# Fifty-four of the input-projection units computed in pairs as Strassen's 2x2 block product

## What is computed

```python
h = rmsnorm(x, norm_g)                                   # 1056 x 1024
p = jnp.einsum('btd,dn->btn', h, w_in)                   # 1024 -> 12296 columns
o_a = silu(a_z) * (a_b * causal_dwconv(a_c * a_u, buf_a, conv_a_w))          # 3 taps
o_r = silu(r_z) * head_norm(retention_chunked(rotary(r_q), rotary(r_k), r_v, s_ret))
conv_c = causal_dwconv(glu_v * sigmoid(glu_g), buf_c, conv_c_w) + conv_c_b   # 31 taps
o_c = silu(c_z) * silu(layernorm(conv_c, ln_c_g, ln_c_b))
o_m = silu(m_z) * head_norm(sigmoid(m_o) * mlstm_chunked(m_q, m_k, m_v, i_pre, f_pre, ...))
proj = jnp.einsum('btnw,nwd->btnd', stack([o_a, o_r, o_c, o_m]), w_br)       # 4 x (512 -> 1024)
gates = sigmoid(g_all.reshape(bsz, T, 4, 1024))
y = jnp.einsum('btd,de->bte', jnp.sum(gates * proj, axis=2), w_out)
out = rmsnorm(x + y, final_g)                            # and the new states
```

## Time and profile before

| | us |
|---|---|
| median of 3 runs | 1593.6 |
| lowest, highest | 1592.13, 1593.8 |
| the profiled execution, whole | 1592.14 |
| its span, first to last instruction | 1590.1 |
| TensorE busy | 1560.0 |
| VectorE busy | 817.2 |
| ScalarE busy | 415.8 |
| GpSimd busy | 385.3 |
| mean granted clock of TensorE, share of full | 0.995 |

### The profile page before, as it was taken

One profiled execution on the slowest core, in us unless ns is written; L12 is line 12 of the kernel. 1 busy time (PEld: TensorE's weight loads), 2 busy tenths in 40 slices (PEclk: granted clock), 3 DMA queues, 4 the chain that ended last, 5 costly groups with the idle time before them and its releaser, 6 DMA issues.

```text
span 1590.1 us, 24807 instructions
## 1 busy us (share of the span) xinstructions
PE 1560.0 (98%) x10217; PEld 1541.0 (97%) x10217; DVE 817.2 (51%) x1571; ACT 415.8 (26%) x756; POOL 385.3 (24%) x213
## 2 busy tenths in 40 slices
PE   8899999999999999999999999999999999999998
PEld 7899999999999999999999999989999999999998
DVE  6553342464100757644475469999947532332432
ACT  5332323233111223234211112121123322211311
POOL 4321212222221221221312322232322124431100
PEclk9999999999999999999999999999999999999999
DMA  4120211211111110221111211111111111221321
GB/s 166 56 96 27 69 45 52 82 34 51 54 47 47 48 64 27 71 72 27 56 47 40 71 44 44 57 47 40 47 42 47 40 54 41 87 77 49 103 84 70
DMA packets 27688, 92.34 MB, mean 58 GB/s; under 512 B 3624, under 2 KB 4152, under 8 KB 27448
## 3 DMA queue, kind: packets, MB, share of 16 engines
q1 hardware_dynamic: 22632, 73.35, 14.2%
q0 software_dynamic: 3744, 13.08, 2.4%
q10 hardware_dynamic: 1200, 4.33, 0.7%
...
## 4 chain that ended last, share of the span: by engine, by line
PE 86%; DVE 9%; issue 3%; ACT 1%; POOL 1%; DMA 0%; DVEq 0%; SPq 0%; ACTq 0%
PE bank L681 24%; PE bank L682 24%; PE bank L683 24%; DVE cc L1738 3%; PE bank L873 2%; PE bank L875 2%; PE bank L874 2%; DVE xt L1318 1%; PE pb L784 1%; PE tb L769 1%; PE pb L802 1%; PE pb L788 1%; PE tb L812 1%; PE pb L787 1%; PE tb L765 0%
## 5 line engine op out<-in xcount | busy, mean ns | idle before, releaser
L681 PE MATMUL bank<-h_hi,w_hi 128*128 128x352 f32 x2328 | 765.5, 329 | 12.6 <-POOL w_lo L1174 4.9
L683 PE MATMUL bank<-h_hi,w_lo 128*128 128x352 f32 x2328 | 749.9, 322 | 0.0
L682 PE MATMUL bank<-h_lo,w_hi 128*128 128x352 f32 x2328 | 749.7, 322 | 0.0
L1174 POOL TENSOR_TENSOR w_lo<-stage,w_hi 128x1024 fp32r<-128x1024 f32 (+1 forms) x131 | 286.3, 2185 | 814.5 <-ACT w_hi L903 814.3
L681 PEld LDWEIGHTS bank<-h_hi,w_hi 128*128 128x128 f32 x2328 | 439.6, 189 | 15.1 <-POOL w_lo L1174 5.4
L682 PEld LDWEIGHTS bank<-h_lo,w_hi 128*128 128x128 f32 x2328 | 440.4, 189 | 0.5
L683 PEld LDWEIGHTS bank<-h_hi,w_lo 128*128 128x128 f32 x2328 | 438.8, 188 | 0.0
L1738 DVE SCALAR_TENSOR_TENSOR cc<-ext,vc,cc 128x1024 f32<-128x1024 f32 x240 | 217.6, 948 | 19.0 <-ACT cc L1100 10.5
L903 ACT ACTIVATE w_hi<-stage 128x1024 fp32r<-128x1024 f32 (+1 forms) x131 | 124.6, 951 | 250.3 <-PE bank L683 239.4
L681 PE MATMUL bank<-o_hi,w_hi 128*128 128x352 f32 x384 | 124.7, 325 | 0.2 <-issue 0.2
L682 PE MATMUL bank<-o_lo,w_hi 128*128 128x352 f32 x384 | 123.3, 321 | 0.0
...
## 6 DMA issues: line engine op xcount, KB each, us to landing
...
```

The lines of the kernel that those rows point to most:

```text
L681: pe.matmul(out, hi, a_hi[:, k, tok(b)], start=(k == 0), stop=False)
L682: pe.matmul(out, hi, a_lo[:, k, tok(b)], start=False, stop=False)
L683: mm = pe.matmul(out, lo, a_hi[:, k, tok(b)], start=False, stop=(k == nk - 1))
L1174: pool.tensor_tensor(lo, stage[n % RING][:, 0:size], hi.bitcast(F32), ALU.subtract).then_inc(lo_done, 1)
```

## The change

**Pairs.** 43 units are computed as before, one after another. The other 54 form 27 pairs; the two units of a pair are the rows of a 2x2 block matrix, the halves of K its columns. The tokens are four blocks of 264 (`SBK`); the two blocks of one half (tp = 0, 1) are the columns of the other matrix. A pair is seven products of 128x512 weights with 512x264 columns for each tp, in the order P1, P6, P5, P7, P2, P4, P3: 14 steps of 12 matmuls. Kinds are "g" (two gates), "cvcg", "acau", "abaz" and "cz".

**Sums.** The combinations of h are made once by DVE (`comb`, `comb4`) and split by ACT and POOL; they take the place of acc and o in SBUF. The sums of weights are made by POOL for each pair (`sums`, four instructions), into `wsum` and in place in `stage`. Six weight slots of 128x512 (`t_hi`, `t_lo`) are a ring over the products. Part of the additions of results happens in PSUM: P2 adds onto P1's bank, P7 and P4 onto P6's, P3 onto P5's; before the next product is added, ACT or DVE must have read the bank (s1 after P1; u2 after P6; u3 and r22 after P7; r21 after P4; r12 after P3). TensorE waits for s1, u2, u3 and r22.

**DRAM.** Finished branch outputs go to DRAM (`store_out`, 16 of 128x1056), gates too (each 128x264 piece from SP as soon as its sigmoid is done). The merge of all 32 "p" units comes behind the pairs (`pblk`, three blocks of 352 each); gate pieces and outputs are loaded again there (`gload`, `oload`).

**Convolution.** One tap every 2.25 product steps, without a gap, steps 0 to 272 of 378; the layer norm's tasks lie at steps 276 to 321.

**Last stage.** Two halves of 512 columns in place of four quarters of 256.

```diff
+SBK = T // 4
...
-    tasks = {}
-    for g in range(1, 4):
-        tasks.update(spread(taps(g), 38 * g - 24, 1.25))
...
+    for what in (glu(1), None, conv_a(0), out_a(0), None, conv_a(1), glu(2), None, out_a(1), None, conv_a(2), glu(3),
+                 None, out_a(2), None, conv_a(3), None, out_a(3), None, None, None, None, None, out_c(0), out_c(2),
+                 None, None):
...
+    for g in range(4):
+        for i in range(1, CW):
+            tasks_at(68 * g + int(2.25 * (i - 1)), *([("tap0", g)] if i == 1 else []), ("tap", g, i))
...
+    cycle = [4, 2 * r0, 2 * r0 + 1, 2 * r1, 2 * r1 + 1, 5]
+    slot_of, prev = {}, {}
+    tiles = [("win", w, i) for w in range(nw) for i in range(7)]
+    for t, tile in enumerate(tiles):
+        slot_of[tile] = cycle[t % 6]
...
-            def split_lo(n):
-                src, dst = SPLITS[n]
-                size = src_of(src).shape[-1]
-                hi, lo = dst_of(dst, size)
-                pool.wait_ge(hi_done, n + 1)
-                pool.tensor_tensor(lo, stage[n % RING][:, 0:size], hi.bitcast(F32), ALU.subtract).then_inc(lo_done, 1)
...
+            def sums(w, pair):
+                first, second = stage_of(("win", w, 0)), stage_of(("win", w, 1))
+                if pair == 0:
+                    loaded(pool, ("win", w, 1))
+                    pool.tensor_tensor(wsum[0][:, :], second[:, 0:W], second[:, W:D], ALU.add).then_inc(wsum_done, 1)
+                    loaded(pool, ("win", w, 0))
+                    pool.wait_ge(wsum_done, 4 * w + 1)
+                    pool.tensor_tensor(wsum[1][:, :], wsum[0][:, :], first[:, 0:W], ALU.subtract).then_inc(wsum_done, 1)
+                else:
+                    pool.tensor_tensor(second[:, 0:W], first[:, 0:W], second[:, 0:W], ALU.subtract).then_inc(wsum_done, 1)
+                    pool.wait_ge(wsum_done, 4 * w + 2)
+                    pool.tensor_tensor(wsum[1][:, :], first[:, W:D], wsum[1][:, :], ALU.subtract).then_inc(wsum_done, 1)
+            def split(s):
+                item = SPL[s]
+                if item[0] == "win" and item[2] == P1:
+                    sums(item[1], 0)
+                hi, lo = dst_of(item)
+                pool.wait_ge(hi_done, s + 1)
+                pool.tensor_tensor(lo, split_src(item), hi.bitcast(F32), ALU.subtract).then_inc(lo_done, 1)
+                if item[0] == "win" and item[2] == P5:
...
+            def store_out(n, src):
+                pool.wait_ge(gated, n + 1)
+                pool.dma_start(o_rows[out_row(n)], src[:, :]).then_inc(o_out, 16)
...
+            def prod(w, i, tp):
+                if PAIRS[w][0] == "g" and signed("g", i):
+                    idx = SIG[(w, SIG_AT[i], tp)]
+                    unit, blk_, _ = GATE_OF[idx]
+                    sp.wait_ge(sgt_ready, idx + 1)
+                    sp.dma_start(g_rows[unit, :, sub(blk_)], sgt[idx % NT][:, :]).then_inc(g_out[idx % NT], 16)
...
+            def gload(x):
+                m, b = divmod(x, 3)
+                n, j = OUTS[m]
+                unit = n * KD + j
...
+                if piece_use(x) > 1:
+                    sp.wait_ge(piece_used, x - (6 if x < 48 else 5) + 1)
+                sp.dma_start(piece[piece_slot(x)][:, :], g_rows[unit, :, tok(b)]).then_inc(piece_in[piece_slot(x)], 16)
...
+            def prod(w, i, tp):
+                kind, n = PAIRS[w][0], 2 * w + tp + 1
+                tile = ("win", w, i)
+                if tp == 0:
+                    pe.wait_ge(lo_done, AT_SPLIT[tile] + 1)
+                nb = {P1: 0, P2: 0, P6: 2, P7: 2, P4: 2, P5: 4, P3: 4}[i] + tp
+                if i in (P1, P6, P5):
+                    take(nb)
+                if i == P6 and w == 0:
+                    pe.wait_ge(comb_lo, 12)
+                if i == P4 and w == 0:
+                    pe.wait_ge(t4_lo, 4)
+                if i == P7:
+                    pe.wait_ge(u2_done, n)
+                if i == P2:
+                    pe.wait_ge(s1_done, n)
+                    if kind == "g":
+                        last[nb] = (sgt_ready, SIG[(w, 11, tp)] + 1)
+                    else:
+                        e, c = FREED[("prod", w, i, tp)]
+                        last[nb] = (freed[e], c)
+                if i == P4:
+                    pe.wait_ge(u3_done, n)
+                    last[nb] = (r21_done, n)
+                if i == P3:
+                    pe.wait_ge(r22_done, n)
+                    last[nb] = (r12_done, n)
+                if i in (P6, P5, P7):
+                    c = {P5: 0, P6: 1, P7: 2}[i]
+                    a_hi, a_lo = (lambda k: c_hi[c][:, k, tp, :]), (lambda k: c_lo[c][:, k, tp, :])
+                else:
+                    k0, lr = {P1: (0, 0), P2: (4, 0), P4: (0, 1), P3: (4, 1)}[i]
+                    a_hi, a_lo = (lambda k: h_hi[:, k0 + k, sub(2 * tp + lr)]), (lambda k: h_lo[:, k0 + k, sub(2 * tp + lr)])
+                out, hi_t, lo_t = bank[nb][:, 0:SBK], t_hi[SLOT_OF[tile]], t_lo[SLOT_OF[tile]]
+                first = i in (P1, P6, P5)
+                for k in range(4):
+                    hi, lo = hi_t[:, k * P:(k + 1) * P], lo_t[:, k * P:(k + 1) * P]
+                    pe.matmul(out, hi, a_hi(k), start=(first and k == 0), stop=False, skip_group_check=True)
+                    pe.matmul(out, hi, a_lo(k), start=False, stop=False, skip_group_check=True)
+                    mm = pe.matmul(out, lo, a_hi(k), start=False, stop=(k == 3), skip_group_check=True)
+                mm.then_inc(blk_done, 1)
...
-                for q in range(4):
-                    out = ring[2 * (i % 4) + q // 2][:, 256 * (q % 2):256 * (q % 2) + 256]
+                for q in range(2):
+                    out = ring[2 * (i % 4) + q][:, :]
...
+            def prod(w, i, tp):
+                kind, info, _ = PAIRS[w]
+                n, done = 2 * w + tp + 1, DONE[("prod", w, i, tp)]
+                a_bank, b_bank, c_bank = (bank[2 * j + tp][:, 0:SBK] for j in range(3))
+                s1, u2, u3 = part[tp][:, :], part[2 + tp][:, :], part[4 + tp][:, :]
+                before = PAIRS[w - 1][0] if w else None
+                even, odd = sub(2 * tp), sub(2 * tp + 1)
+                if i == P6:
+                    dve.wait_ge(blk_done, done)
+                    dve.wait_ge(s1_done, n)
+                    if before == "g":
+                        dve.wait_ge(sgt_ready, SIG[(w - 1, 12, tp)] + 1)
+                    TT(u2, b_bank, s1, ALU.add).then_inc(u2_done, 1)
+                elif i == P7:
+                    dve.wait_ge(blk_done, done)
+                    if before in ("g", "cvcg"):
+                        dve.wait_ge(sgt_ready, SIG[(w - 1, 22, tp)] + 1)
+                    if w == 0:
+                        for s in gp_out:
+                            dve.wait_ge(s, 16 * (3 * PLAIN_GATES // 2))
+                    TT(u3, b_bank, s1, ALU.add).then_inc(u3_done, 1)
+                    dve.wait_ge(u3_done, n)
+                    TT(u3, c_bank, u3, ALU.add).then_inc(r22_done, 1)
...
+                elif i == P4:
+                    dve.wait_ge(blk_done, done)
+                    TT(s1, b_bank, s1, ALU.add).then_inc(r21_done, 1)
...
+                dve.wait_ge(blk_done, done)
+                TT(u2, c_bank, u2, ALU.add).then_inc(r12_done, 1)
+                if kind == "g":
+                    return
...
+            def pblk(m, b):
+                x = 3 * m + b
+                n, j = m // KD, OUTS[m][1]
+                ps, gate = bank[x % BANKS][:, 0:BLK], piece[piece_slot(x)][:, :]
+                dve.wait_ge(blk_done, DONE[("pblk", m, b)])
+                dve.wait_ge(piece_in[piece_slot(x)], 16 * piece_use(x))
+                if n == 0:
+                    own(TT(acc[:, j, tok(b)], ps, gate, ALU.mult))
+                    own.wait()
                     dve.sem_inc(freed["V"], 1)
-                    if b == 2:
-                        dve.wait_ge(olo_done, 8 + g)
...
-    wo = arr(w_out)[0].reshape(2, 4, P, 4, 256).transpose(3, 0, 2, 1, 4).reshape(8, P, D)
+    wo = arr(w_out)[0].reshape(4, 2, P, 2, 512).transpose(3, 0, 2, 1, 4).reshape(8, P, D)
```

1091 lines of the change are left out of this document (751 added, 340 removed).

## The result

The changed kernel takes **1675.97 us** (median of four runs, 1674.34 to 1678.09) against 1593.62: the ratio is 1.052, 95% interval 1.0501 to 1.0538. The prediction gave 1668 us, within 1588 to 1728. The profiled run has a span of 1672.6 us.

What follows compares the result with a forecast made beforehand. TensorE bounds the kernel before; in the pairs VectorE, slowed by GpSimd, would. 1592.1 - 70.8 (TensorE's work) + 138 (waiting for VectorE) + 8 (layer norm) = 1667, given as 1668 us, range 1588 to 1728.

Steps and rivals of the forecast that it cites:

- TensorE's own work: Matmuls of the 27 pairs and the last stage: fewer or cheaper, saving 67.3 and 3.5 us, together -70.8 us.
- VectorE undisturbed: Pairs up to step 272: VectorE's work without GpSimd's interference is 337 us, hidden under TensorE's 395 us.
- What a pair loses to GpSimd: In the pairs GpSimd's 14.1 us cost VectorE 10.3 us a pair, ratio 0.73; 7.0 by the lower ratio 0.49.
- the first rival: In the pairs VectorE loses under 3.0 us a pair, TensorE stays the bound: 1526 us, chance 0.18.
- The difference to TensorE: Pairs up to step 272: VectorE needs 537 us against TensorE's 395, 142 more, less 4 slack: +138 us.
- Layer norm: Steps 276 to 321: VectorE's work there, contended by GpSimd, adds 8 us, bounds 0 and +20.
- Clock: Half-speed stretches where TensorE waits for VectorE are mostly waiting turned into work: 0, bound +30 us.
- Taken at nothing, the combinations: The four combinations of h hide under plain units; only the first pair's P4 block may cost 0 to 3 us.
- Waits by place: In the pairs TensorE waits for VectorE's u2 and u3, several us a pair, up to the last tap.
- Merge and DMA: In the merge six banks cover VectorE's work; reading gate pieces is the heaviest new traffic, bound 0 to +10 us.
- break-even of 6.8: In the pairs the change turns from gain to loss at 6.8 us of VectorE time lost a pair.
- The third rival: Every GpSimd instruction costs VectorE its whole time, 14.1 us a pair: 1753 us, chance 0.14.

Runs made afterwards that it cites:

- e_comb2: Changed kernel with the first three quarters' combinations of h at the end of their attention phases and the first pair's P4 block five steps earlier: 1651.13 us.
- e_sum16: Changed kernel with GpSimd's four weight sums of a pair on 16 of 512 columns (full in the first pair only), low parts full: 1608.24 us.
- e_psum: Changed kernel with the 31-tap convolution summed in two free PSUM banks, sample columns done once per group, taps starting four steps later: 1598.00 us.

## Why the prediction was right, and which steps were not

The mechanism is the one foretold: GpSimd's doubled load takes time from VectorE, VectorE needs more than TensorE, and TensorE waits for it at u2. The size of the total is partly luck, as the terms show.

**TensorE's own work** (-67.3 and -3.5): right. The same count at the edges as above makes 158.5 and 117.1 ns of the earlier trace rows 159.0 and 117.5 from start to start. A pair then cost 144 x 159.0 = 22.90 us and costs 168 x 121.6 = 20.43 (20.33 predicted): 67 us gained. In the last stage 432 matmuls of 232.5 ns are 100.4 us and 864 of 117.5 were 101.5: 1.1 gained for 3.5.

**VectorE undisturbed** (337 us up to step 272): 299 measured, 38 too high. The additions and the branch products were costed too dearly, from undisturbed sizes plus a gap for each. Queued behind each other they overlap: an addition of results costs 0.39 us from start to start for the 0.49 predicted, which is 21 of the 38 us; the rest lies in the products.

**What a pair loses to GpSimd** (10.3 us, ratio 0.73): 8.5 us, ratio 0.60, between the two ratios that the earlier trace rows had given. The reason given for the higher one, that VectorE would be as full as in the dense stretch, nearly came true (464.6 of 514 us, 90%, against 93%), so it doesn't explain the difference. That the dense stretch had longer GpSimd instructions, as the first rival says, was not tested; the cause stays open.

**The difference to TensorE** (+142, and +138 with the slack): by work alone 464.6 - 19.43 x 20.52 = 66 us. The stage up to step 272 took 514, 115 over. The missing 49 us are VectorE's own idle time in the stage, which the prediction's picture of a saturated engine left out. It waits for ScalarE's first tap when the group changes (2.45, 2.5 and 5.7 us), once 10.6 us for TensorE, and many times in small pieces. That it also waits for TensorE's half clock behind each lump is likely, not shown.

**Layer norm** (+8, bounds 0 and +20): wrong, too small. Steps 276 to 321 took 94.9 us (1202.5 to 1297.4) for 67 us of matmuls, 28 us over and outside the bounds. The stretch of it that holds the waits, all engines:

```profile
1197.00:1290.00 93.00, 78.05 (x575) 75.49 (x574) 55.55 (x82) 41.22 (x77) 48.11 (x36) 0.92 0.21 71
```

TensorE waits 4.6, 4.3, 2.1, 1.5 and 2.7 us from 1220 on, 15 us, and 20 us of the stretch are at half clock. VectorE is busy for only 56 of the 93 us: here the waits come from single steps that are late, not from too much work. Over all 27 pairs the surplus is 115 + 28 = 143 us where the prediction's terms give 138 + 8: one 23 us too high, the other 20 too low.

**Clock** (0, bound +30): wrong. "Waiting turned into work" would leave 102 us of waits as the whole surplus; 41 us stand beside them. So a VectorE undisturbed and a loss to GpSimd costed too high stood against an idle VectorE, the slow clock and the layer norm left out or too low, and they nearly cancelled.

**Taken at nothing, the combinations**: wrong by 25 us (e_comb2), and the bound of 0 to 3 us looked at the wrong end, the last block before P4. Most of it arises in the middle of the attention, through ScalarE's order. That the total doesn't show it has this reason: the sum carried along the whole 199 us of the kernel before that are neither units nor last stage. 9 us of waits behind 679, some 3 us for the half clock behind two of them, and 1.6 us that the last stage took above its pitch belonged to the part that the change replaced.

**Waits by place**: u2 as foretold, u3 hardly, most likely since whoever was late had been waited for at P7. **Merge and DMA** (0 to +10): 184.9 us for 182.6, at 199 GB/s, +2.

**The rivals.** The first (TensorE stays the bound, 1526 us) needed a loss under 3.0 us a pair; it was 8.5. Its break-even of 6.8 stays untested: e_sum16 loses 5.5 a pair and is still 1% slower than the kernel before, but the combinations' 25 us account for more than that. What e_sum16 does show is that 76 us of waits and slow clock remain in its pairs although VectorE's need is level with TensorE's: a sum of needs says nothing of waits of single pairs, which the three-tap convolution and branch A's products make. The third rival (the whole 14.1 us) is out by the 0.60. The exclusive lock that the Trainium skill states ("SBUF — State Buffer", Who interferes with whom) against VectorE instructions with two SBUF inputs is borne out in kind by e_psum. If every GpSimd instruction cost VectorE its whole time, 274 us would be lost where 165 were: two fifths of GpSimd's time cost VectorE nothing. That it fell beside reads of PSUM and idle time is the likely reason; it was not taken apart.
